# Hybrid encoder trunk: two operands turned by VectorE blocks and a trip through memory instead of by TensorE

## The reference, cut to what matters

```python
h = rms_norm(x, norm_g) * (1 + scale) + shift
proj = h @ w_in                                  # (256 tokens, 13824 columns)
pool_u, pool_z, q, k, v, attn_z, conv_a, conv_b, conv_z, gates = split(proj)

# pooling: per group of 256 channels, trailing mean over w = 2, 4, 8, 16 tokens, minus the token
mixed = (cs - shifted(cs, w)) / cnt - ug         # along tokens
y_pool = einsum('bsgc,gcd->bsgd', mixed, pool_w) * pool_scale * silu(pool_z)

# convolution: GLU, causal depthwise convolution of width 31 along tokens, LayerNorm, SiLU, pointwise
g = conv_a * sigmoid(conv_b)
y = depthwise(pad(g, 30), dw) + dw_b
y_conv = (silu(layer_norm(y)) @ conv_pw) * silu(conv_z)

merged = g_pool * (y_pool @ w_bp) + g_attn * (y_attn @ w_ba) + g_conv * (y_conv @ w_bc)
out = rms_norm(x + gate * (merged @ w_out)) 
```

## Time and profile before

| | us |
|---|---|
| median of 3 runs | 942.22 (942.02 to 943.11) |
| the profiled execution, time | 942.33 |
| its span, first to last instruction | 940.5 |
| around the span (942.33 - 940.5) | 1.8 |
| PE busy within the span | 911.0 (97%) |
| DVE busy | 703.0 (75%) |
| ACT busy | 420.6 (45%) |
| POOL busy | 9.2 (1%) |

### The profile page before, as it was taken

One profiled execution on the slowest core, in us unless ns is written; L12 is line 12 of the kernel. 1 busy time (PEld: TensorE's weight loads), 2 busy tenths in 40 slices (PEclk: granted clock), 3 DMA queues, 4 the chain that ended last, 5 costly groups with the idle time before them and its releaser, 6 DMA issues.

```text
span 940.5 us, 10296 instructions
## 1 busy us (share of the span) xinstructions
PE 911.0 (97%) x4211; PEld 732.9 (78%) x4211; DVE 703.0 (75%) x794; ACT 420.6 (45%) x388; POOL 9.2 (1%) x26
## 2 busy tenths in 40 slices
PE   1999999999999999999999999999999999999996
PEld 1667777888888888888877777888888888888885
DVE  4778787878968777767688786685687988865783
ACT  3445252645344334444375655347433443444332
POOL 2000000000000000000000000000000000000000
PEclk9999999999999999999999999999999999999999
DMA  9999999855446556555545456656879998955512
GB/s 337 387 386 386 385 332 388 311 179 179 160 155 213 189 182 208 193 179 179 183 138 171 139 159 149 208 171 153 271 241 394 374 335 276 352 207 191 182 45 90
DMA packets 108208, 220.01 MB, mean 234 GB/s; under 512 B 3858, under 2 KB 3938, under 8 KB 107393
## 3 DMA queue, kind: packets, MB, share of 16 engines
q1 hardware_dynamic: 106768, 213.15, 67.1%
q0 software_dynamic: 1104, 5.42, 1.5%
q10 hardware_dynamic: 288, 0.79, 0.2%
HBM read 217.24 MB, written 2.10 MB: 233 GB/s over the span
## 4 chain that ended last, share of the span: by engine, by line
PE 90%; DVE 4%; DMA 3%; ACT 2%; issue 1%; SPq 0%; DVEq 0%; ACTq 0%
PE acc_odd L1246 13%; PE acc_odd L1248 13%; PE acc_odd L1247 13%; PE acc_even L1246 12%; PE acc_even L1248 12%; PE acc_even L1247 12%; PE side_a L1246 2%; PE side_a L1248 2%; PE side_a L1247 2%; PE side_b L1306 2%; DMA raw<-in_w_ada 1%; DVE gate_sums L1089 1%; DMA x_tok<-in_x 1%; PE side_b L1246 1%; PE side_a L1291 1%
## 5 line engine op out<-in xcount | busy, mean ns | idle before, releaser
L759 DVE TENSOR_TENSOR wl<-raw,wh 128x2048 fp32r<-128x2048 f32 x147 | 336.0, 2290 | 147.8 <-ACT wh L466 147.5
L466 ACT ACTIVATE wh<-raw 128x2048 fp32r<-128x2048 f32 x147 | 280.2, 1913 | 261.3 <-PE acc_odd L1248 105.7
L1246 PE MATMUL acc_odd<-wh,act_h 128*128 128x512 f32 x432 | 169.8, 393 | 0.0
L1246 PE MATMUL acc_even<-wh,act_h 128*128 128x512 f32 x430 | 169.7, 395 | 0.0
L1247 PE MATMUL acc_odd<-wl,act_h 128*128 128x512 f32 x432 | 168.2, 389 | 0.0
L1248 PE MATMUL acc_odd<-wh,act_l 128*128 128x512 f32 x432 | 168.2, 389 | 0.0
L1248 PE MATMUL acc_even<-wh,act_l 128*128 128x512 f32 x430 | 167.6, 390 | 0.0
L1247 PE MATMUL acc_even<-wl,act_h 128*128 128x512 f32 x430 | 167.4, 389 | 0.0
L974 DVE SCALAR_TENSOR_TENSOR conv_slots<-conv_slots,taps 128x256 f32<-128x256 f32 x240 | 100.2, 479 | 0.2
L1246 PEld LDWEIGHTS acc_even<-wh,act_h 128*128 128x128 f32 x430 | 80.7, 188 | 19.5 <-issue 2.8
L1246 PEld LDWEIGHTS acc_odd<-wh,act_h 128*128 128x128 f32 x432 | 81.1, 188 | 18.9 <-issue 2.2
(11 more groups left out here) (294 smaller groups left out, 925.8 us busy)
## 6 DMA issues: line engine op xcount, KB each, us to landing
raw<-in_w_in SPq DMA_DIRECT2D x106, 1024.0 KB, 5.1
raw<-in_w_ada SPq DMA_DIRECT2D x48, 1024.0 KB, 9.3
raw<-in_w_out SPq DMA_DIRECT2D x16, 1024.0 KB, 5.0
raw<-in_w_branch_pool SPq DMA_DIRECT2D x8, 1024.0 KB, 5.0
raw<-in_w_branch_attn SPq DMA_DIRECT2D x16, 512.0 KB, 6.7
raw<-in_w_branch_conv SPq DMA_DIRECT2D x8, 1024.0 KB, 6.4
raw<-in_conv_pw SPq DMA_DIRECT2D x4, 1024.0 KB, 5.9
x_tok<-in_x SPq DMA_DIRECT2D x2, 1024.0 KB, 9.2
```

The costliest lines, as they stand in the source:

```text
L466: nc.scalar.activation(wh[:, m % RING], raw[SLOT_OF[g]][:, :, :], ACT.Copy).then_inc(high_done, 1)
L759: nc.vector.tensor_tensor(wl[:, m % RING], raw[SLOT_OF[load_of(m)]][:, :, :], wh[:, m % RING].bitcast(F32), ALU.subtract).then_inc(raw_don ...
L1246: nc.tensor.matmul(sums, xh, wh[:, slot, i, :], start=begin, stop=False)
```

## The change

Four results are no longer turned by PE. For each, DVE now makes two transposes of 128x512 that turn every 32x32 block in place (`turn_blocks`), into a new buffer `blocks[name]`. POOL then stores the buffer to a scratch tensor in device memory with four DMAs, one for each group of 32 partitions (`store_blocks`), waits for all four, and loads it back with four DMAs of 128 rows of 1 KB (`load_turned`), straight into `conv_slots` or `pool_in`. The four results go through POOL one after the other: glu0, u0, u1, glu1. In a store, the 32 floats of a row of a block lie together in memory, 512 bytes from the next, so each of the four DMAs writes 1024 runs of 128 bytes.

PE loses four times eight transposes and the waits ahead of them, ACT four copies of 128x1024. The taps start in step 27 instead of 26 and end in 88; the pooling's windows, products, gating and turning all come one step or one piece later. ACT's step 31 gets a wait for the landing of glu1, since glu1's block buffer and `pool_silu[1]` share their place.

```diff
-TAPS_AT = {m: 4 for m in range(26, 88)}
+TAPS_AT = {m: 4 for m in range(27, 89)}
+TURNS = ("glu0", "u0", "u1", "glu1")
+    blocks = {name: at(f"blocks_{name}", [P, 4, 4, TH, QUAD], F32, offset * KB)
+              for name, offset in (("glu0", 176), ("u0", 180), ("u1", 184), ("glu1", 188))}
+    scratch = {name: nc.dram_tensor(f"turned_{name}", (QUAD, 4, 4 * TH, 4, QUAD), F32, kind="Internal").ap()
+               for name in TURNS}
...
+            def store_blocks(name):
+
+                pool.wait_ge(blocks_ready, TURNS.index(name) + 1)
+                for a_ in range(4):
+                    pool.dma_start(scratch[name].rearrange("j b n a i -> j (b n) a i")[:, :, a_, :],
+                                   blocks[name][QUAD * a_:QUAD * (a_ + 1), :, :, :, :].rearrange("j b t h i -> j (b t h) i")
+                                   ).then_inc(blocks_stored, 16)
+                pool.wait_ge(blocks_stored, 16 * 4 * (TURNS.index(name) + 1))
+
+            def load_turned(name, dst):
+                for t in range(4):
+                    pool.dma_start(dst[:, t, :], scratch[name].rearrange("j b (t h) a i -> t b j (h a i)", t=4)[t]
+                                   ).then_inc(turned[name], 16)
+
+            store_blocks("glu0")
+            load_turned("glu0", conv_slots[:, 2:6, TAPS - 1:SLOT])
+            store_blocks("u0")
+            load_turned("u0", pool_in[:, 0:4, PAD:PAD + SEQ])
+            store_blocks("u1")
+            load_turned("u1", pool_in[:, 4:8, PAD:PAD + SEQ])
+            store_blocks("glu1")
+            load_turned("glu1", conv_slots[:, 6:10, TAPS - 1:SLOT])
...
-                if m == 24:
-                    act.wait_ge(pads_ready, 1)
-                    spread(conv_slots[:, 2:6, TAPS - 1:SLOT], by_tiles(pb), glu_t, 1, glu_copied)
-                if m == 27:
-                    spread(conv_slots[:, 6:10, TAPS - 1:SLOT], by_tiles(pa), glu_t, 2, glu_copied)
...
-                    spread(pool_in[:, 0:4, PAD:PAD + SEQ], by_tiles(pb), u_t, 1, u_copied)
-                if m == 30:
-                    spread(pool_in[:, 4:8, PAD:PAD + SEQ], by_tiles(pa), u_t, 2, u_copied)
                 if m == 31:
+                    act.wait_ge(turned["glu1"], 64)
                     evacuate("zp1", pool_silu[1][:, :, :], ACT.Silu)
...
+            def turn_blocks(name, src):
+
+                for h in range(TH):
+                    last = nc.vector.transpose(blocks[name][:, :, :, h, :].rearrange("p b t i -> p t b i"),
+                                               src[:, h, :].rearrange("p (t b j) -> p t b j", t=4, b=4))
+                last.then_inc(blocks_ready, 1)
...
                 if i == 0:
-                    dve.wait_ge(glu_copied, 1)
+                    dve.wait_ge(pads_ready, 1)
+                    dve.wait_ge(turned["glu0"], 64)
                 if pair == 2 and rest == 0:
-                    dve.wait_ge(glu_copied, 2)
+                    dve.wait_ge(turned["glu1"], 64)
...
             def pool_windows(i):
-                dve.wait_ge(u_copied, i + 1)
+                dve.wait_ge(pads_ready, 1)
+                dve.wait_ge(turned[f"u{i}"], 64)
...
-                if m in (30, 32):
-                    pool_windows((m - 30) // 2)
+                if m in (31, 33):
+                    pool_windows((m - 31) // 2)
...
-                if m == 24:
-                    pe.wait_ge(*freed("a0"))
-                    pe.wait_ge(mod_ready, 4)
-                    transpose4(pb, block_of(glu_a[0]), glu_t)
...
-                if m in (32, 34):
-                    pool_mix((m - 32) // 2)
+                if m in (33, 35):
+                    pool_mix((m - 33) // 2)
```

More of the change, by code:

```diff
@@ L271, in program @@
         h_full, h_high, h_ready = sem("h_full"), sem("h_high"), sem("h_ready")
-        glu_ready, glu_t, glu_copied = sem("glu_ready"), sem("glu_transposed"), sem("glu_copied")
+        glu_ready = sem("glu_ready")
+        blocks_ready, blocks_stored = sem("blocks_ready"), sem("blocks_stored")
+        turned = {name: sem(f"turned_{name}") for name in TURNS}
         conv_dve, ln_partial = sem("conv_dve"), sem("ln_partial")
@@ L278, in program @@
         pw_gated = sem("pw_gated")
-        u_t, u_copied, mixed_ready = sem("u_transposed"), sem("u_copied"), sem("mixed_ready")
+        mixed_ready = sem("mixed_ready")
         pool_mm, pool_z_used = sem("pool_mm"), sem("pool_z_used")
@@ L631, in _ @@
                     nc.scalar.activation(pool_silu[0][:, :, :], part["zp0"][:, :, :], ACT.Silu).then_inc(part_silu, 1)
-                    spread(pool_in[:, 0:4, PAD:PAD + SEQ], by_tiles(pb), u_t, 1, u_copied)
-                if m == 30:
-                    spread(pool_in[:, 4:8, PAD:PAD + SEQ], by_tiles(pa), u_t, 2, u_copied)
                 if m == 31:
+                    act.wait_ge(turned["glu1"], 64)
                     evacuate("zp1", pool_silu[1][:, :, :], ACT.Silu)
-                if m in (35, 37):
-                    b = (m - 35) // 2
+                if m in (36, 38):
+                    b = (m - 36) // 2
                     act.wait_ge(y_t, 1 + b)
@@ L1120, in _ @@
                                             ).then_inc(acc_free[NUM["a0"] % 2], 1)
+                    dve.wait_ge(*freed("a0"))
+                    turn_blocks("glu0", glu_a[0][:, :, :])
                 if m in (23, 24, 25, 26, 27):
                     last_part(OPEN[m - 21])
+                if m in (25, 26):
+                    dve.wait_ge(part_done, m - 22)
+                    turn_blocks(f"u{m - 25}", part[f"u{m - 25}"][:, :, :])
                 if m == 26:
@@ L1126, in _ @@
                                             ).then_inc(glu_ready, 1)
-                if m in (30, 32):
-                    pool_windows((m - 30) // 2)
-                if m in (33, 35):
-                    pool_gated((m - 33) // 2)
-                if m in (36, 38):
-                    b = (m - 36) // 2
+                    dve.wait_ge(glu_ready, 1)
+                    turn_blocks("glu1", glu_a[1][:, :, :])
+                if m in (31, 33):
+                    pool_windows((m - 31) // 2)
+                if m in (34, 36):
+                    pool_gated((m - 34) // 2)
+                if m in (37, 39):
+                    b = (m - 37) // 2
                     dve.wait_ge(y_high, 1 + b)
@@ L1405, in pool_mix @@
                 pe.wait_ge(pool_w_loaded, 16)
-                pe.wait_ge(u_copied, i + 1)
+                pe.wait_ge(turned[f"u{i}"], 64)
                 dst = (pb, pa)[i]
@@ L1481, in _ @@
                 piece(*lhs, PK * i, m, sums_of(name), first, i == pieces - 1)
-                if m == 24:
-                    pe.wait_ge(*freed("a0"))
-                    pe.wait_ge(mod_ready, 4)
-                    transpose4(pb, block_of(glu_a[0]), glu_t)
-                if m == 27:
-                    pe.wait_ge(glu_ready, 1)
-                    transpose4(pa, block_of(glu_a[1]), glu_t)
-                if m == 28:
-                    pe.wait_ge(part_done, 3)
-                    pe.wait_ge(glu_copied, 1)
-                    transpose4(pb, block_of(part["u0"]), u_t)
-                if m == 30:
-                    pe.wait_ge(part_done, 4)
-                    pe.wait_ge(glu_copied, 2)
-                    transpose4(pa, block_of(part["u1"]), u_t)
-                if m in (32, 34):
-                    pool_mix((m - 32) // 2)
-                if m == 35:
+                if m in (33, 35):
+                    pool_mix((m - 33) // 2)
+                if m == 36:
                     pe.wait_ge(pool_z_used, 1)
                     transpose4(pb, block_of(zs_pool, 0), y_t)
-                if m == 37:
+                if m == 38:
                     pe.wait_ge(pool_z_used, 2)
```

## The result

The changed kernel takes **944.26 us** (median of 20 runs, 943.15 to 946.4) beside 942.24 for the kernel before, measured together with it (20 runs, 941.62 to 943.11): a ratio of **1.0022 [1.0015, 1.0029]**. The forecast was 938.7, faster; it became slower by 2.0 us: little, but clear of the noise, as the interval lies above 1.

What follows compares the result with a forecast made beforehand. PE's own instruction sequence was taken to bound the kernel: 942.33 profiled minus 3.6 us of PE work, all other terms at cost 0, gave 938.7 us. The range was 938.0 to 950, with 0.64 on 938.0 to 940.3.

Steps and rivals of the forecast that it cites:

- What bounds the kernel, and what PE loses: PE's own instruction sequence sets the time; pieces 24 to 31 shrink from 47.16 to 43.60 us, 3.6 us shorter.
- DVE's transposes: Eight added on DVE in steps 22, 25 and 26, 0.68 us each, 5.4 in all, fitting its gaps and lead: cost 0.
- SP's queue: Stores and loads add 4 MB against 220 beside SP's loads, which have about four pieces of time: cost 0.
- The store S: On POOL, from a block buffer being ready until all four store DMAs are seen done: 7.5 us taken.
- The bound of 9.0: A store on POOL as three issues of 0.94 plus a landing like the pooling weights' 6.2: 9.0 us.
- T: Time when glu1's loads have landed, for which ACT's step 31 waits: 233.5 us on the new clock.
- The chain from S to PE: Three trips in series after u0 on POOL, then ACT, splits and DVE's windows (16.3 us) before PE's second pooling products.
- The limit of T: Latest landing of glu1 without a PE stall: 239.4 us, 5.9 us to spare; reached with stores of 9.5 us.
- the first two rivals: Long POOL stores bring glu1 late and hold ACT and PE; chances 0.20 (slower kernel) and 0.09 (gain partly given back).
- the second rival: Part of the gain given back: stores of 10.0 to 11.2 us, glu1 1.8 to 5.3 late, 940.4 to 944.0; chance 0.09.
- The rule on short transfers: Transfers under 512 bytes miss line rate, which speaks against POOL's stores in 128-byte runs; taken as a rival, chance 0.20.
- the first rival: Short runs are slow: stores beyond 10.7 us make the kernel slower, 959 us at 15.5 per store; chance 0.20 (above 944).

Runs made afterwards that it cites:

- the filled version: The changed kernel with 12 matmuls of 128x512 without use on PE ahead of the second pooling products: 942.34 us, 1.0 of the kernel before.
- the loads without use: The kernel before with 32 DMAs of 128 rows of 1 KB added on POOL's queue, all loads from x, no stores: 942.56 us, 1.0005.
- the second measurement: The changed kernel without any edit, measured and profiled once more: 943.66 us (10 runs), 1.001 of the kernel before.
- the kernel with longer stores: The changed kernel with a fifth DMA in each store, into a spare scratch tensor: 945.35 us, 1.0031 of the kernel before.

## Why the prediction was wrong, step by step

**What bounds the kernel, and what PE loses: right.** 43.52 for eight pieces against 43.60 forecast, 3.6 us less. With the wait out of the way, all of it reaches the end: 938.91 and 938.74 where 938.7 was forecast.

**DVE's transposes: right.** 1.30 for two back to back, 0.65 each where 0.68 was taken, and free.

**SP's queue: right.** The trips beside the kernel before cost nothing measurable, though SP's loads land 2 to 3 us later.

**The store S: wrong, and this is the step that failed.** 7.5 was taken, between 5.5 and 9.0; 9.24 to 10.83 was measured. The row chosen was POOL's own load of the pooling weights, 6.2 us from issue to landing, and I scaled it down because the DMA engines are less busy at the change's place and the stores carry an eighth of the bytes. The runs show that neither made a store quick. Bytes hardly count: alone, a store of this kind is over after 5.6. And the lighter load was that of the kernel without the trips. With them the DMA engines are as busy during the stores (0.80 to 1.05) as they were for the pooling weights (0.98). Both company and short runs then cost more than the stores alone show: long runs instead of short ones take 1.2 off a store alone and 1.5 to 4.3 in the kernel. What is left of the difference between long runs in the kernel (5.25 to 8.86) and alone (4.5 to 4.7) is company; how it is made up was not taken apart further. The bound of 9.0, taken from that row without scaling, would have been nearest. It was in the range for S, and what it gives for T was worked out as 238.0, in time by 1.4 only. A step whose error comes three times over and has 2 us to its limit should not have been given 64 in 100.

**The chain from S to PE: right, but for the loads' issue.** The limit of T was 239.4: at 239.34 PE waits for nothing, at 242.28 for 2.7 (2.9 by that limit), at 243.87 for 4.3 (4.5). From T to the end of the windows it took 16.1 where 16.3 was worked out. One smaller term was short: issuing four loads took 2.7 to 2.9 where 2.3 was taken. With the measured stores and loads the sum of the prediction gives 200.8 + 30.0 + 2 x 2.8 + 6.0 = 242.4 for T. Of the 8.8 us that T came late, the three stores are 7.5 (30.0 - 3 x 7.5) and the loads' issue 1.4. The mechanism is the one that the first two rivals share. By the mean of the last three stores, 10.0, it is the second rival, part of the gain given back with S from 10.0 to 11.2, at 940.4 to 944.0, which was given 0.09; the median of 944.26 lies just above that, for the reason that comes next.

**What the sum left out: the clock.** Even with T known, 938.7 + 2.9 is 941.6, and the median is 2.7 higher. The prediction counted a late T one for one and put nothing for a slower PE behind the wait. In the first trace 1.5 of it is the half clock after the wait, as the filled version shows (0.6 of waiting, no drop) and the twice traced changed kernel (the same wait with and without). Behind the last product another 0.2 goes, in which the span's end and what lies around the span move against each other (8.34 + 2.35 in place of 8.65 + 1.83). The trips and the transposes, each by itself, leave the sum at 10.5; the loads without use have 10.85 (9.02 + 1.83), and in the kernel with longer stores it is 10.15 (8.38 + 1.77). What causes it stays open. The last 1.1 us, from the profiled 943.15 to the median 944.26, has no trace. The mean granted clock tends to be lower in the longer of the 20 runs, 0.996 at 943.15 and 0.993 at 945.27, 945.62 and 946.4, though 0.997 at 944.93. In the ten runs of the second measurement the two shortest (940.57 and 942.0) are the only ones at 0.998. So more time at the half clock is likely, and slower stores beside it; this is inferred.

**The rule on short transfers.** The short runs do cost something: 1.2 us per store alone (5.63 against 4.47), 1.0 to 2.5 beside one load (7.67 and 8.87 against 6.41 and 6.68) and 1.5 to 4.3 in the kernel, and with the long ones PE no longer waits. The Trainium skill, "DMA: Bandwidth & Descriptors", Specifications, says that transfers under 512 bytes miss line rate. The measurement agrees in direction, but not that the rate is the reason: alone, a store's last issue ends 2.5 before it is over with short runs (5.63 - 3.11) and with long ones (4.47 - 2.00) alike. What the short runs cost was enough to decide this case, since there were only 2 us of S to lose. It did not make the first rival's 959 true. The fit of the same page (Anatomy of one DMA) gives an estimated 2.3 us for a DMA of 128 KB; alone 2.46 was measured with long runs and 2.91 with short ones, and beside one load the median of all the stores' DMAs was 4.9.

## What to carry to other kernels

When results go one after the other through a trip that waits for its own landing, an error in the trip's price is multiplied by the number of trips; take the price from a DMA that had company, and put the trip for which an in-order engine waits ahead of those that nobody needs yet, or take away the wait's reason by another buffer. Look up what is queued behind such a wait: here a buffer shared with `pool_silu` cost 5 us, and an order of four names or one offset brought them back. A stall of a PE that sets the time costs more than its length when the clock drops behind it, as in one of the two traces of this kernel.

## What the runs showed of the hardware

- After 2.68 us without a product PE had a granted clock of 0.50 from 258 to 260 and 1.00 again from 262 in one execution, and 16 products took 4.78 instead of 3.27; after 2.71 us it stayed at 1.00 in another of the same kernel; after 4.26 us, in the kernel with longer stores, it was halved again.
- A POOL store of 4 x 128 KB took 5.6 us alone, 7.7 to 8.9 with one 1 MB load of SP's at a time beside it, and 9.2 to 10.8 in the kernel (up to 11.7 with another order of the trips).
- While these trips ran, SP's 1 MB loads landed after 7.9 us (median) instead of 5.1.
- 1024 runs of 128 bytes cost 0.77 us of issue on POOL and 32 runs of 4 KB 0.52, alone and beside SP's loads alike.
- DVE turns all 32x32 blocks of 128x512 f32 in 0.65 us when two follow each other (0.67 to 0.71 each by its own record), as fast as an addition of that shape (0.68).
